# Twelve transformer phases on one core: the output gate turned on TensorE and written to DRAM as rows, late constants and compression weights loaded elsewhere

## Chip, cores, metric

One of the eight cores of a Trainium2 chip. The metric is the device time of one execution in microseconds (us), as the median of several runs. All data is float32.

## The reference

Four blocks of three sublayers each run over 256 tokens of width 1024, twelve sublayers (phases) in all, one after the other. Each adds to the residual x a gated result:

```python
mod = (silu(c) @ ada_w[l] + ada_b[l]).reshape(B, 3, 3, 1, D)     # shift, scale, gate of each sublayer
n = rmsnorm(x, norm_g[l, j]) * (1 + mod[:, j, 1]) + mod[:, j, 0]
x = x + factor * gate(mod[:, j, 2]) * sublayer(n)                # factor 0.5 for j = 0 and 2, else 1
```

gate is 1 + mod in blocks 0 and 1, and mod itself in blocks 2 and 3. Sublayers j = 0 and j = 2 are SwiGLU FFNs, (silu(n @ wi_gate) * (n @ wi_up)) @ wo, with hidden width 2816. Sublayer j = 1 is a mixer: HGRN2 (block 0), differential attention (block 1), and in blocks 2 and 3 native sparse attention beside a spatial-gating MLP. The sparse attention compresses its keys and values with small weights (cmp_w1, cmp_w2). A final rmsnorm ends it. The gate of a sublayer is a vector of 1024 numbers, one for each output channel, the same for all tokens.

## The kernel before

**Phases.** PHASES lists (l, j) for l = 0..3, j = 0..2. (l, 0) and (l, 2) are FFNs, eight in all; (l, 1) are the mixers.

**Weights.** All weights stream from DRAM in pieces of 1 MB (128 x 2048), each as two DMAs of 512 KB, through a ring of three slots, raw. `load` (L354) waits on s_split until the slot's old piece has been cut. For each piece ScalarE copies raw to its high part wH (L504), and VectorE subtracts to get the low part wL (L875), which releases the slot. TensorE then computes each product in three matmuls: high x high (L1530), high x low weights (L1532), low x high (L1534). The last piece of an FFN goes to its own buffers lastH and lastL (L511, L882). All DMAs are issued by the SP queue in program order, so whatever SP waits for holds back everything behind it.

**An FFN.** The hidden width is taken in NF = 11 chunks of 256. A turn takes three pieces: two up pieces (the halves of the contraction over 1024) and one down piece. In turn k TensorE does up(0) for chunk k, then turn_hidden (L1574, four transposes of the hidden chunk k-1 into TM), up(1) for chunk k, and down of chunk k-1. ScalarE copies the turned chunk to hH (L584), and VectorE makes hL (L1010). Chunk 0 and turn 1 are written out, turns 2 to 9 are a hardware loop, turn 10 is written out again, token tile by token tile: turn_hidden, a token tile of up(1), a down tile, turn_tile(0) (L1610), the other token tile, down_last(0), turn_tile(1), a down tile, down_last(1). ScalarE's order there is: cut of up, cut of down chunk 9, cut_last of down chunk 10, hidden_high, cut of the next phase's first piece, then the silu of tile 0 (L592). VectorE's product of tile 0 (L1016) is what turn_tile(0) waits for.

**Modulation.** mod is computed on the side. Matrices of 2 MB a turn (ada, two DMAs of 1 MB) are multiplied with the condition on VectorE (L888), in up to ten turns of an FFN. Each such chunk gives 4 of the 72 columns of a block; a gate takes two chunks.

**The gate.** VectorE computes it as a column tile gcol [128, 8] (gate_column, L932 or L934): element d * 128 + p lies in partition p, column d. The kernel needs it the other way, the same 1024 numbers along the free axis in all partitions (gB [128, 1024]). It goes through DRAM: gate_out (L368) writes gcol to a row of the DRAM tensor gates, and gate_in (L377) waits for that write to land (s_gd), and for the earlier phase's outputs, and reads the row into all 128 partitions:

```python
sp.dma_start(T["gates"][n - 1].rearrange("(d p) -> p d", p=P), gcol[:, :],
             allow_slow_non_contiguous=True).then_inc(s_gd, 16)
```

The order p, d against (d p) makes each of the 1024 elements of four bytes a piece of its own. In an FFN the SP queue has: the loop's loads (the last is the down piece of chunk 9), gate_out, the down piece of chunk 10, gate_in, then the loads of the next phase. In a mixer gate_out stands before the seventh piece and gate_in before the eleventh.

**Late constants** (L416 to L422): a table of 1286 KB, the positions as 256 elements of four bytes, and four vectors read into all partitions. They are issued in (0,0) behind the loop, ahead of gate_out. VectorE waits for them in the first mixer.

**Compression and spatial weights** of blocks 2 and 3 (L476 to L480): cmp_w1 as two DMAs of 1 MB, cmp_w2, gm_ws and two vectors. They are issued ahead of the mixer's first piece.

## Time and profile before

| | |
|---|---|
| median of 3 runs | 2505.46 us (2504.33 to 2522.29) |
| the profiled execution's own time | 2514.27 us |
| its span, first to last instruction | 2512.5 us |
| mean granted TensorE clock | 0.945 of full |
| busy, share of the span: TensorE, VectorE, ScalarE | 91%, 66%, 44% |
| DMA | 537.72 MB, mean 214 GB/s |

An execution's time is its span and 1.8 us around it. PE is the matmuls of TensorE, PEld its weight loads, which overlap them; DVE is VectorE, ACT ScalarE, SPq the queue of SyncE that issues the DMAs. TensorE's matmuls are pipelined, so that a busy PE is not PE at its peak. In a waits row, the engine on the left was idle until the one on the right was done.

### The profile page before, as it was taken

To read this page: it belongs to the slowest core of one execution; us is meant where nothing else is said; L and a number is where in the kernel's file an instruction comes from. 1 tells how busy PE (TensorE), PEld (TensorE's weight loads), DVE (VectorE), ACT (ScalarE), POOL (GpSimd) and SP (SyncE) were. 2 spreads that over 40 slices of the span, in tenths; PEclk is the share of its full clock that TensorE was granted. 3 is DMA by queue.
4 is the path that set the end of the run, shared out by engine and by line. 5 is a ranking of instruction groups with operands and counts; after the bars stand their busy time and mean duration, and the time that the engine had idled before them with its cause. 6 is when DMAs were issued, how large, how long until landed. Compare 5 with 4: busy or idle time off the path is not lost.

```text
span 2512.5 us, 30163 instructions
## 1 busy us (share of the span) xinstructions
PE 2274.6 (91%) x10812; PEld 1888.1 (75%) x10812; DVE 1655.6 (66%) x2305; ACT 1095.3 (44%) x1289; POOL 0.2 (0%) x4
## 2 busy tenths in 40 slices
PE   4997895899899896999899798999989979899998
PEld 3886784688788774788788587778878868777886
DVE  6875667877687686676677554477757756446455
ACT  3443644443444455444433354553444335464433
POOL 0000000000000000000000000000000000000000
PEclk9998997999999996999999897899999989799999
DMA  7987630688698650687698652249768884223554
GB/s 298 332 310 211 165 129 17 227 328 308 198 331 313 200 175 35 217 326 248 189 332 311 209 144 84 101 175 333 284 186 297 308 290 128 101 101 118 184 191 127
DMA packets 140656, 537.72 MB, mean 214 GB/s; under 512 B 27424, under 2 KB 28192, under 8 KB 121504
## 3 DMA queue, kind: packets, MB, share of 16 engines
q1 hardware_dynamic: 140576, 536.64, 62.7%
q8 instruction: 52, 0.85, 0.1%
q14 instruction: 28, 0.23, 0.0%
HBM read 535.49 MB, written 1.10 MB: 214 GB/s over the span
## 4 chain that ended last, share of the span: by engine, by line
PE 73%; DVE 11%; DMA 7%; ACT 6%; issue 2%; SPq 1%; ACTq 0%; DVEq 0%
PE GU L1530 12%; PE GU L1534 11%; PE GU L1532 11%; PE PY L1530 9%; PE PY L1532 9%; PE PY L1534 9%; DVE wL L875 4%; DMA gates<-gcol 3%; ACT wH L504 3%; PE TM L1574 1%; DMA raw<-in_c_w 1%; DMA raw<-in_up_w 1%; PE PY L1777 1%; DVE ada L888 1%; PE PY L1874 1%
## 5 line engine op out<-in xcount | busy, mean ns | idle before, releaser
L875 DVE TENSOR_TENSOR wL<-raw,wH 128x2048 fp32r<-128x2048 f32 x344 | 777.0, 2279 | 284.5 <-ACT wH L504 283.7
L504 ACT ACTIVATE wH<-raw 128x2048 fp32r<-128x2048 f32 x344 | 645.1, 1900 | 237.2 <-PE PY L1534 94.8
L1530 PE MATMUL GU<-wH,xH 128*128 128x512 f32 (+1 forms) x1600 | 640.5, 400 | 40.6 <-DVE xL L997 31.6
L1534 PE MATMUL GU<-wH,xL 128*128 128x512 f32 (+1 forms) x1600 | 627.6, 392 | 0.0
L1532 PE MATMUL GU<-wL,xH 128*128 128x512 f32 (+1 forms) x1600 | 626.9, 392 | 0.0
L1530 PEld LDWEIGHTS GU<-wH,xH 128*128 128x128 f32 x1600 | 304.9, 191 | 109.4 <-issue 29.5
L1534 PEld LDWEIGHTS GU<-wH,xL 128*128 128x128 f32 x1600 | 304.5, 190 | 64.8
L1532 PEld LDWEIGHTS GU<-wL,xH 128*128 128x128 f32 x1600 | 305.3, 191 | 58.8
L888 DVE CUSTOM_DVE_ANT_0 ada<-ada,cond 128x1024 f32<-128x1024 f32 x272 | 316.7, 1221 | 0.0
L584 ACT ACTIVATE hH<-TM 128x512 fp32r<-128x512 f32 x80 | 47.7, 597 | 581.5 <-PE TM L1574 581.5
L1530 PE MATMUL PY<-wH,hH 128*128 128x512 f32 x640 | 203.3, 399 | 39.6 <-DVE hL L1010 38.4
L1010 DVE TENSOR_TENSOR hL<-TM,hH 128x512 fp32r<-128x512 f32 x80 | 55.3, 692 | 239.8 <-ACT hH L584 239.6
L1534 PE MATMUL PY<-wH,hL 128*128 128x512 f32 x640 | 201.3, 396 | 0.0
L1532 PE MATMUL PY<-wL,hH 128*128 128x512 f32 x640 | 200.9, 396 | 0.0
L1530 PE MATMUL PY<-wH,xH 128*128 128x512 f32 x432 | 178.2, 412 | 9.5 <-DVE wL L875 8.1
L1532 PE MATMUL PY<-wL,xH 128*128 128x512 f32 x432 | 173.4, 401 | 0.0
L1534 PE MATMUL PY<-wH,xL 128*128 128x512 f32 x432 | 172.9, 400 | 0.0
L1530 PEld LDWEIGHTS PY<-wH,hH 128*128 128x128 f32 x640 | 120.5, 191 | 69.2 <-issue 41.6
L1534 PEld LDWEIGHTS PY<-wH,hL 128*128 128x128 f32 x640 | 122.6, 192 | 26.2
L1532 PEld LDWEIGHTS PY<-wL,hH 128*128 128x128 f32 x640 | 122.5, 191 | 26.2
L1530 PEld LDWEIGHTS PY<-wH,xH 128*128 128x128 f32 x432 | 85.1, 197 | 29.4 <-issue 5.5
L1534 PEld LDWEIGHTS PY<-wH,xL 128*128 128x128 f32 x432 | 84.2, 195 | 18.6
(293 smaller groups left out, 2079.6 us busy)
## 6 DMA issues: line engine op xcount, KB each, us to landing
raw<-in_up_w SPq DMA_DIRECT2D x352, 512.0 KB, 6.3
ada<-in_ada_t SPq DMA_DIRECT2D x136, 1024.0 KB, 7.9
raw<-in_down_w SPq DMA_DIRECT2D x176, 512.0 KB, 4.7
raw<-in_c_w SPq DMA_DIRECT2D x96, 512.0 KB, 4.5
raw<-in_a_w SPq DMA_DIRECT2D x40, 512.0 KB, 4.5
raw<-in_b_w SPq DMA_DIRECT2D x32, 512.0 KB, 4.8
M<-in_ada_t SPq DMA_DIRECT2D x8, 1024.0 KB, 12.3
gB<-gates SPq DMA_DIRECT2D x12, 512.0 KB, 5.8
```

Source lines behind the costliest of these rows:

```text
L504: act.activation(wH[:, to, 0:words], raw[:, slot, 0:words], ACT.Copy).then_inc(s_high, 1)
L584: act.activation(hH[:, :, :].rearrange("p f s -> p (f s)"), TM[:, 0, :], ACT.Copy).then_inc(s_hh, 1)
L875: dve.tensor_tensor(wL[:, to, 0:words], raw[:, slot, 0:words], wH[:, to, 0:words], ALU.subtract).then_inc(s_split, 1)
L888: ins = dve.tensor_tensor_reduce(w, w, cond[:, :], 1.0, 0.0, ALU.mult, ALU.add, acc[:, 2 * q + b:2 * q + b + 1])
L1010: dve.tensor_tensor(hL[:, :, :].rearrange("p f s -> p (f s)"), TM[:, 0, :], hH[:, :, :].rearrange("p f s -> p (f s)"), ALU.subtract).then_ ...
L1530: pe.matmul(outs[i], aH, wh[i], start=first, stop=False)
L1532: pe.matmul(outs[i], aH, wl[i], start=False, stop=False)
L1534: ins = pe.matmul(outs[i], aL, wh[i], start=False, stop=last)
L1574: ins = pe.transpose(TM[:, 0, f * S + i * P:f * S + (i + 1) * P], sh[:, 1, i, f * P:(f + 1) * P], ident)
L1777: ins = pe.matmul(banks[:, 2 * c + n, 0:P * (tile + 1)], queries[r, h, tile * P:(tile + 1) * P], keys(h)[r, 0:P * (tile + 1)], start=True, ...
L1874: ins = pe.matmul(PY[:, 2, 64 * j:64 * j + 33], w, cT_[:, j, n % 8, n // 8:n // 8 + 33], start=(n == 0), stop=(n == 15))
```

## The change

- gcol has 16 columns. gate_columns takes gate_column's place: in (l, 0) it computes the gates of (l, 0) and (l, 1) at once, in (l, 2) its own. It stands behind the eighth turn of the loop; the mixers compute none.
- In each FFN one more turn is written out of the loops of PE and ACT, turn 9 (the tenth, with chunk 0). After its turn_hidden PE transposes gcol into bank 1 of TM, as 8 or 16 rows of 128; ACT copies that to a new tile gT. DVE's last loop turn becomes a piece of its own as well.
- gate_out writes gT: rows of 128 numbers, 512 bytes, 16 for (l, 0) and 8 for (l, 2). It waits for ACT's copy (s_grow). There are eight such writes; those of the mixers are gone. gate_in reads as before.
- The late constants are issued behind the fifth of (0,0)'s ten ada turns.
- In blocks 2 and 3 the compression weights are issued ahead of the mixer's fifth piece, behind a wait for the outputs of (l, 0), and the spatial weights ahead of the eighth.

```diff
-            def gate_out():
-                n = t.next("gate")
-                sp.wait_ge(s_gcol, n)
-                sp.dma_start(T["gates"][n - 1].rearrange("(d p) -> p d", p=P), gcol[:, :],
-                             allow_slow_non_contiguous=True).then_inc(s_gd, 16)
+            def gate_out(l, j):
+                sp.wait_ge(s_grow, t.next(s_grow))
+                n, rows = 3 * l + j, 2 if j == 0 else 1
+                sp.dma_start(T["gates"][n:n + rows].rearrange("n (d p) -> (n d) p", p=P), gT[0:rows * ND, :]
+                             ).then_inc(s_gd, 16)
...
+            def gate_in(l, j):
+                n = 3 * l + j
+                sp.wait_ge(s_gd, 16 * (2 * l + 1 + j // 2))
+                if n:
+                    sp.wait_ge(s_x, NT * n)
+                sp.dma_start(gB[:, :], T["gates"][n:n + 1].broadcast_to([P, D])).then_inc(s_gb, 16)
+            def load_compression(i):
+                sp.wait_ge(s_x, NT * (3 * i + 7))
+                for k in range(2):
+                    sp.dma_start(w1_[k], T["cmp_w1"][i, k]).then_inc(s_w1, 16)
+                sp.dma_start(w2_[:, :, :], T["cmp_w2_2"][i].rearrange("j f d -> f j d")).then_inc(s_w1, 16)
...
-                    if n == 6:
-                        gate_out()
                     if n == 10:
-                        gate_in()
+                        gate_in(l, 1)
+                    if l > 1 and n == 4:
+                        load_compression(l - 2)
+                    if l > 1 and n == 7:
+                        load_spatial(l - 2)
...
-                if turns:
+                if (l, j) == (0, 0):
+                    loop(1, 5, 1)
+                    late_constants()
+                    loop(6, turns - 5, 1, c0 + 5)
+                elif turns:
                     loop(1, turns, 1)
-                if (l, j) == (0, 0):
-                    late_constants()
...
-                loop(NF - 2)
+                loop(NF - 3)
+                cut()
+                hidden_high()
+                rows = 2 * ND if j == 0 else ND
+                act.wait_ge(s_gt, t.next(s_gt))
+                act.activation(gT[0:rows, :], TM[0:rows, 1, 0:P], ACT.Copy).then_inc(s_grow, 1)
+                cut()
+                cut()
+                silu_gate()
...
+            def gate_columns(l, j):
+                for k in range(2 if j == 0 else 1):
+                    m = (3 * l + j + k) * 3 * ND
+                    factor = 1.0 if k else 0.5
+                    gate, to = mod[:, m + 2 * ND:m + 3 * ND], gcol[:, k * ND:(k + 1) * ND]
...
-                gate_column(l, j)
...
+                loop(NF - 3, turns > 0)
+                gate_columns(l, j)
+                if turns == NF - 1:
+                    c0 = c0 + NF - 3
+                    loop(1, 1)
+                    c0 = c0 + 1
+                else:
+                    loop(1, 0)
...
-                loop(NF - 3)
+                loop(NF - 4)
+                pe.wait_ge(s_h, t.next(s_h))
+                up(0)
+                turn_hidden()
+                rows = 2 * ND if j == 0 else ND
+                pe.wait_ge(s_gcol, t.next(s_gcol))
+                pe.transpose(TM[0:rows, 1, 0:P], gcol[:, 0:rows], ident).then_inc(s_gt, 1)
+                up(1)
+                down(False)
```

The SP queue at the end of (0,0), before; the names are DRAM tensor (in_...) or tile, to<-from, and the semaphores waited for stand in brackets:

```order
L416 DMA cst<-in_table 128x2572
L417 DMA posi<-in_positions 128x2x1
L422 DMA vb<-in_a_onorm 128x128
L422 DMA M<-in_b_qk_g 128x128
L422 DMA M<-in_b_subln 128x128
L422 DMA M<-in_b_lam 128x256
L368 DMA gates<-gcol 128x8x1 [waits s_gcol]
L354 DMA raw<-in_down_w 128x1024 [waits s_split]
L354 DMA raw<-in_down_w 128x1024
L377 DMA gB<-gates 128x1024 [waits s_gd]
L354 DMA raw<-in_a_w 128x1024 [waits s_split]
```

The same place in the changed kernel:

```order
L371 DMA gates<-gT 16x128 [waits s_grow]
L357 DMA raw<-in_down_w 128x1024 [waits s_split]
L357 DMA raw<-in_down_w 128x1024
L380 DMA gB<-gates 128x1024 [waits s_gd]
L357 DMA raw<-in_a_w 128x1024 [waits s_split]
```

The constants have left (they stand between the two loops now), and the gate write takes 16 rows of 128 and waits for s_grow.

ScalarE from the end of its loop to the last cut of (0,0), in the changed kernel (before, the loop is followed at once by the last three of these rows):

```order
L516 ACTIVATE wH<-raw 128x2048 [waits s_eaten,s_raw1]
L596 ACTIVATE hH<-TM 128x512 [waits s_ht]
L637 ACTIVATE gT<-TM 16x128 [waits s_gt]
L516 ACTIVATE wH<-raw 128x2048 [waits s_eaten,s_raw2]
L516 ACTIVATE wH<-raw 128x2048 [waits s_eaten,s_raw0]
L587 ACTIVATE sh<-GU 128x512 [waits s_eaten]
L516 ACTIVATE wH<-raw 128x2048 [waits s_eaten,s_raw1]
L516 ACTIVATE wH<-raw 128x2048 [waits s_eaten,s_raw2]
L523 ACTIVATE lastH<-raw 128x2048 [waits s_raw0]
```

The first six rows are the tenth turn, which was the loop's last; the copy to gT stands between hidden_high and two cuts.

The SP queue at the start of the mixer of block 2, in the changed kernel:

```order
L380 DMA gB<-gates 128x1024 [waits s_x,s_gd]
L357 DMA raw<-in_c_w 128x1024 [waits s_split]
L357 DMA raw<-in_c_w 128x1024
...
L357 DMA raw<-in_c_w 128x1024 [waits s_split]
L357 DMA raw<-in_c_w 128x1024
L386 DMA M<-in_cmp_w 128x2048 [waits s_x]
L386 DMA M<-in_cmp_w 128x2048
L387 DMA w_<-in_cmp_w_2 128x2x64
L357 DMA raw<-in_c_w 128x560 [waits s_split]
```

The first two of the weights M<-in_cmp_w stood directly behind gB<-gates before; now four pieces are ahead of them, and a wait for s_x.

## Rows read from the trace of the kernel before

**Rows 1.** The page: busy time, and the chain by engine.

```profile
PE 2274.6 (91%) x10812; PEld 1888.1 (75%) x10812; DVE 1655.6 (66%) x2305; ACT 1095.3 (44%) x1289; POOL 0.2 (0%) x4
...
PE 73%; DVE 11%; DMA 7%; ACT 6%; issue 2%; SPq 1%; ACTq 0%; DVEq 0%
```

**Rows 2.** Waits: waiting <- waited for: us in total, times, longest us.

```profile
ACT lastH L511 <- DMA raw<-in_down_w: 51.6, 8, 16.2
...
SPq L377 <- DMA gates<-gcol: 82.6, 8, 13.2
```

**Rows 3.** Windows: one loop turn of (0,0); start:end length, then the columns named.

```profile
core 0: us, PE busy (x) PEld busy (x) DVE busy (x) ACT busy (x) POOL busy (x), PEclk, DMA share, GB/s
144.80:161.60 16.80, 16.80 (x78) 13.91 (x77) 12.72 (x15) 6.61 (x5) 0.00 (x0) 1.00 0.86 314
```

**Rows 4.** Windows: ends of the eight FFNs, last turn_hidden to last matmul.

```profile
213.54:249.33 35.79, 20.50 (x83) 15.93 (x82) 12.50 (x18) 10.56 (x15) 0.00 (x0) 0.76 0.63 164
641.72:666.99 25.27, 19.62 (x83) 15.30 (x82) 12.51 (x18) 10.56 (x15) 0.00 (x0) 0.93 0.89 288
841.33:867.36 26.03, 20.90 (x83) 16.12 (x82) 12.48 (x18) 10.56 (x15) 0.00 (x0) 0.87 0.55 191
1200.56:1225.79 25.23, 20.34 (x83) 15.93 (x82) 12.51 (x18) 10.56 (x15) 0.00 (x0) 0.86 0.83 291
1400.38:1437.09 36.71, 22.39 (x83) 17.56 (x82) 13.64 (x18) 12.48 (x16) 0.00 (x0) 0.77 0.63 229
1843.63:1870.56 26.93, 20.84 (x83) 16.38 (x82) 11.35 (x17) 10.56 (x15) 0.00 (x0) 0.87 0.74 268
2044.94:2079.47 34.53, 21.75 (x83) 16.88 (x82) 13.32 (x18) 10.57 (x15) 0.00 (x0) 0.80 0.68 243
2484.94:2505.24 20.30, 17.82 (x81) 14.04 (x79) 10.90 (x16) 6.85 (x13) 0.00 (x0) 1.00 0.29 85
sum 230.79, PE 164.17 PEld 128.14 DVE 99.22 ACT 82.69 POOL 0.00; mean PE 20.52 PEld 16.02 DVE 12.40 ACT 10.34 POOL 0.00
```

**Rows 5.** Timeline, end of (0,2): start, us, engine, line, operation, count, [idle before <- releaser].

```profile
630.45 0.85 SPq L354 DMA_DIRECT2D raw<-in_down_w  x2
...
631.52 0.38 SPq L368 DMA_DIRECT2D gates<-gcol  x1
...
632.51 0.82 SPq L354 DMA_DIRECT2D raw<-in_down_w  x2
...
633.48 2.29 DVE L875 TENSOR_TENSOR wL<-raw,wH 128x2048 fp32r<-128x2048 f32 x1 [0.33 <-ACT wH L504]
...
641.72 0.60 PE L1574 MATMUL TM<-cst,sh 128*128 128x128 f32 x4
...
644.37 0.33 SPq L377 DMA_DIRECT2D gB<-gates  x1
...
646.09 1.91 ACT L511 ACTIVATE lastH<-raw 128x2048 fp32r<-128x2048 f32 x1 [7.64 <-DMA raw<-in_down_w]
...
649.36 0.70 PE L1530 MATMUL PY<-wH,hH 128*128 128x512 f32 x2 [4.28 <-DVE hL L1010]
...
652.61 1.91 ACT L504 ACTIVATE wH<-raw 128x2048 fp32r<-128x2048 f32 x1 [4.12 <-DMA raw<-in_up_w]
...
655.30 0.44 PE L1610 MATMUL TM<-cst,sh 128*128 128x128 f32 x2 [1.36 <-DVE sh L1016]
```

**Rows 6.** Landing of the down pieces issued at 630.45 and at 632.51, us.

```profile
DMA to landing us min/median/max: 4.0/4.4/4.8
...
DMA to landing us min/median/max: 12.3/12.7/13.2
```

**Rows 7.** Chain of waits at the end of (0,2): the next phase's first piece.

```profile
645.22 7.37 DMA raw<-in_up_w
```

**Rows 8.** DMA issues: count, KB each, median us to landing.

```profile
cst<-in_table SPq DMA_DIRECT2D x1, 1286.0 KB, 7.2
...
out<-x SPq DMA_DIRECT2D x2, 512.0 KB, 2.6
```

More of the change, by code:

```diff
@@ L168, in build @@
         scl = sb("scl", [P, ND])
-        gcol = sb("gcol", [P, ND])
+        gcol = sb("gcol", [P, 2 * ND])
+        gT = sb("gT", [2 * ND, P])
         acc = sb("acc", [P, 4])
@@ L273, in build @@
         s_gcol = sem("s_gcol")
+        s_gt = sem("s_gt")
+        s_grow = sem("s_grow")
         s_gd = sem("s_gd")
@@ L362, in load_down, with load_spatial @@
                 load(T["down_w"][l, j // 2][bass.ds(c, 1)].rearrange("c p n -> p (c n)"))
-            def gate_out():
-                n = t.next("gate")
-                sp.wait_ge(s_gcol, n)
-                sp.dma_start(T["gates"][n - 1].rearrange("(d p) -> p d", p=P), gcol[:, :],
-                             allow_slow_non_contiguous=True).then_inc(s_gd, 16)
-            def gate_in():
-                n = t.next("gate", 0)
-                sp.wait_ge(s_gd, 16 * n)
-                if n > 1:
-                    sp.wait_ge(s_x, NT * (n - 1))
-                sp.dma_start(gB[:, :], T["gates"][n - 1:n].broadcast_to([P, D])).then_inc(s_gb, 16)
+            def gate_out(l, j):
[14 more added lines that the diff above has]
+                sp.dma_start(w2_[:, :, :], T["cmp_w2_2"][i].rearrange("j f d -> f j d")).then_inc(s_w1, 16)
+            def load_spatial(i):
+                sp.dma_start(ws_, T["gm_ws"][i].rearrange("t (g s) -> t g s", s=P)).then_inc(s_gm, 16)
+                for k, name in enumerate(("gm_ln_g_2", "gm_ln_b_2")):
+                    sp.dma_start(ln_[:, k, :], T[name][i].unsqueeze(0).broadcast_to([P, 512])).then_inc(s_gm, 16)
             def load_mixer(w, pieces, l):
@@ L432, in ffn, with loop @@
                 c0, turns = ada_turns(l, j)
-                def loop(first, count, with_ada):
+                def loop(first, count, with_ada, c=c0):
                     with sp.Fori(0, count) as i:
@@ L472, in _ @@
                 else:
[L473 to L481 removed]
+                    load_mixer(T["c_w"][l - 2], PIECES_C, l)
             if len(PHASES) == 12:
@@ L618, in loop @@
                     t.leave(count)
-                loop(NF - 2)
+                loop(NF - 3)
[7 more added lines that the diff above has]
+                silu_gate()
+                t.next("done")
                 cut()
@@ L924, in columns @@
                 dve.wait_ge(s_scl, t.next(s_scl))
-            def gate_column(l, j):
-                m = (3 * l + j) * 3 * ND
-                factor = 0.5 if j != 1 else 1.0
-                gate = mod[:, m + 2 * ND:m + 3 * ND]
-                if l < 2:
-                    dve.tensor_scalar(gcol[:, :], gate, 1.0, factor, ALU.add, ALU.mult).then_inc(s_gcol, 1)
-                else:
-                    dve.tensor_scalar(gcol[:, :], gate, factor, None, ALU.mult).then_inc(s_gcol, 1)
+            def gate_columns(l, j):
[3 more added lines that the diff above has]
+                    gate, to = mod[:, m + 2 * ND:m + 3 * ND], gcol[:, k * ND:(k + 1) * ND]
+                    if l < 2:
+                        ins = dve.tensor_scalar(to, gate, 1.0, factor, ALU.add, ALU.mult)
+                    else:
+                        ins = dve.tensor_scalar(to, gate, factor, None, ALU.mult)
+                ins.then_inc(s_gcol, 1)
             def chunk(c):
@@ L1050, in loop @@
                     t.leave(count)
-                done = 0
-                if l == 0:
-                    loop(2, 1)
-                    done, c0 = 2, c0 + 2
-                gate_column(l, j)
-                more = min(turns, NF - 2) - done
-                if more:
-                    loop(more, 1)
-                    done, c0 = done + more, c0 + more
-                if done < NF - 2:
-                    loop(NF - 2 - done, 0)
+                loop(NF - 3, turns > 0)
[4 more added lines that the diff above has]
+                    c0 = c0 + 1
+                else:
+                    loop(1, 0)
                 cut()
@@ L1496, in _ @@
                 boundary(l, j, before, pieces)
-                if j == 1:
-                    gate_column(l, j)
                 if j != 1:
```

17 lines of the change are left out of this document (4 added, 13 removed).

## The prediction

> **What bounds the kernel now.** I read the page's busy line and its chain first, then the waits, then the ends of the eight FFN phases as windows, and last one such end as a timeline.
>
> The page gives TensorE 91% of the span, and the chain is 73% PE [rows 1]. The same line has 7% DMA, and a DMA in the chain of a kernel whose loads are meant to run ahead is something to ask about. The waits answer it [rows 2]: ScalarE waits 51.6 us in 8 cases for the last down piece (lastH), and the SP queue waits 82.6 us in 8 cases for gates<-gcol before it may issue gB<-gates. There are 8 FFN phases, and each has one of either; the other 4 of the 12 gate writes, those in the mixers, are waited for by nobody.
>
> So the loop turns are one thing and the ends of the phases another. In a loop turn PE is busy all 16.80 us at the full clock [rows 3]: nothing gained there on another engine helps. The windows from the last full turn_hidden of a phase to the end of its last matmul [rows 4] have the same work each time, 72 matmuls of 512 columns and 8 transposes (the window counts 83 with neighbours at its edges). They last 20.30 to 36.71 us, 230.79 us together.
>
> What this work takes when nothing holds it: the last window is 20.30 us, at clock 1.00, and PE's busy time in it is 17.82. A loop turn is also 72 matmuls, with 4 transposes; four transposes take 0.60, in the row at 641.72 [rows 5], so 16.80 + 0.60 = 17.4. I take 17.85 as the floor of one end. Eight of them are 142.8, and 230.8 - 142.8 = **88.0 us** are idle time and lowered clock. The other seven windows show PEclk 0.76 to 0.93: of the two levels, 2.4 and 1.2 GHz, the lower one is granted for a part of them, after PE stood idle. That belongs to the 88.0 and goes with the idle time.
>
> **Why these ends are long.** Phase (0,2) is the plain case [rows 5]. SP issues the down piece of chunk 9 at 630.45, the gate write at 631.52 and the down piece of chunk 10 at 632.51. The first lands after 4.4 us, the last after 12.7 [rows 6], with the 1024 four-byte elements of the gate write between them. lastH therefore starts at 646.09, hH and hL behind it, and PE stands 4.28 us before 649.36. Meanwhile SP stands until 644.37, when the gate write has landed (12.85 us after its issue), and only then issues gB and the next phase's first piece. The half issued at 645.22 lands 7.37 later [rows 7], ScalarE's cut of it runs at 652.61, the silu and the product queue behind that, and PE stands again, 1.36 before 655.30.
>
> **The change, part by part.**
>
> *Gate as rows.* Eight writes instead of twelve, of 8 or 16 rows of 512 bytes instead of 1024 or more separate elements. The trace has no such write. Bounds for its landing, G, from its issue: from below, the only other write to DRAM, out<-x with 512 KB, lands in 2.6 us on an empty queue [rows 8], and here 4.2 us are left until the down piece ahead of it is in (630.97 + 4.8 - 631.52); from above, today's 12.85. The write differs from out<-x in being 100 times smaller and from today's in having 64 or 128 times fewer elements, so I stand near the lower end: G about 5.
>
> Then the end of (0,2) goes like this. Down chunk 10 lands near 637.5 (as its neighbour, within 4.8). ScalarE cuts it before 640, ahead of PE's turn_hidden at 641.72, so hH and hL are there when PE asks (it needs hL only after the 12 matmuls of a token tile, 2.7 us later). That wait is gone. What is late next is the next phase's first piece. PE reaches turn_tile at 641.72 + 0.36 + 2.7 + 2.7 = 647.5; from landing to that point today takes 655.30 - 652.59 = 2.7, so the piece must land by 644.8. It lands at 631.52 + G + 0.86 + 7.37 = 639.75 + G, hence in time for G up to 5.1. I take 0.5 us of remaining wait for each of the 7 phases that have a successor: 3.5 us. For G = 12.85 nothing but the queueing of the down piece would be gained.
>
> The Trainium skill bears on G. The page DMA: Bandwidth & Descriptors (Queues, rings and completion order) says that a DMA's semaphore increment is an ordered write, which lands only after every earlier write of that DMA engine. That would be why a 4 KB write holds back whoever waits behind it, and it sets the same 4.2 us under G. The same page (Latency and other measured facts) puts a fixed cost of about 2 us on a DMA because of the round trip of its receipt. Were that to come on top, an estimate from the page is G = 6.2 and 1.1 us of wait in each of 7 phases, and the sum would be some 4 us higher than mine. No run here shows that for such a write yet.
>
> *The hand-over DVE, PE, ACT, SP.* gate_columns stands behind turn 8's product; PE waits for it only after up(0), some 5 us later, so it waits for nothing. On PE 8 transposes are added in a stretch without slack: 0.15 each by the four for 0.60, 1.2 us in all (bounds: 0 and, if each is drained before the next matmul, 0.6 x 8 = 4.8). ACT's copy of 128 columns is under the 0.60 of the 512-column one, and in a loop turn ACT is busy 6.61 of 16.80 [rows 3]. If that cover were gone it would cost 8 x 0.3 = 2.4. Behind it wait two cuts, whose halves DVE takes 1 us later. SP waits for s_grow before the gate write, and behind it stand the last down piece and gB; the copy is done about 5 us before SP arrives there (turn_hidden of that turn is 16.8 before 641.72, SP arrives at 631.4). 0.
>
> *Mixers.* Four gate writes leave the SP queue; nobody waited for them [rows 2], and the pieces behind them were not what PE waited for. 0, at best a few us.
>
> *Late constants* go from the end of (0,0) to behind its fifth turn. The end of (0,0) is 35.79 against 25.27, 26.03 and 25.23 of the three with no such loads [rows 4]: 10.3 us, part of the 88.0 already. What they cost at the new place: the DMA engines are busy 0.86 there [rows 3], so the 1286 KB table (7.2 us to landing [rows 8]) delays the next pieces. Upper bound 10.3 as at the old place; lower 0. What covers it: a piece's low half is ready at 633.48 + 2.29 = 635.8 and PE asks for it after 641.72, 6 us of slack [rows 5]. One table's delay is about that. I take 1.
>
> *Compression weights* go from ahead of the next phase's first piece to behind its fourth. They are in the two windows of 36.71 and 34.53, again within the 88.0. At the new place 2 MB are issued while the DMA queue is nearly empty, well ahead of their first use; 0, at most 3 each.
>
> **Sum.** -88.0 + 3.5 + 1.2 + 1.0 = -82.3 us. The profiled execution took 2514.27 us (span 2512.5 and 1.8 around it), so the changed one would take 2432.0. The median of the runs, 2505.46, lies 8.8 below the profiled execution; carried over, 2423.2. The idle parts may be a little shorter in an unprofiled run, so I say 2425.
>
> **Rivals.**
>
> *A second slow link remains.* The reads right behind gB stay slow, or G is 8.5: the first piece of the next phase is then 3.4 late in 7 phases, 24 instead of 3.5: 2445. For it: gB itself reads one 4 KB row 128 times. Against it: my 7.37 was measured with gB ahead.
>
> *The write is as slow as before*, because what is slow is a write among reads, not the small element. Then only the constants (10.3) and the compression weights (36.71 + 34.53 - 2 x 25.5 = 20.2) give anything: 2505.5 - 30.5 + 2.2 = 2477. For it: every gate write in the trace is of four-byte elements, so the two can't be told apart. Against it: out<-x.
>
> *Slower: PE waits for instructions.* The tenth turn is now written out, some 60 more PE instructions in each of 8 phases, fetched by the DMA engines that the loads keep 0.86 busy. If each needs a fetch that queues like the down piece of [rows 6], 12.7 us, this is 102 us, and 2525. It decides from 88 / 8, about 10 us a phase. Against it: PE already leaves its loop for written-out code 8 times and goes from turn to end without a pause (no idle is shown at 641.72). The Trainium skill, Runtime: NRT & Kernel Launch (Instruction fetch mechanics), says that straight-line code is fetched ahead and that taken branches are what stalls, which would make this rival 0 us; the trace agrees as far as it goes.
>
> **How the numbers follow.** Forecast 0.70, second slow link 0.16, write as slow as before 0.10, slower 0.02, something else of no account 0.02. A measurement of this kernel tells about 1% (25 us) from no change. All but the last two are faster by more: faster 0.96, same 0.02, slower 0.02. The range: below, no wait left and no cost of constants, 2505.5 - 88.0 + 1.2 = 2418.7, and a few us from the mixers, 2411; above, the second slow link with the upper bound of the constants and of the transposes in part, 2451. What it leaves out is the 2477 and the slower case.
>
> **What would show it.** In the changed profile the eight windows should be 17.5 to 19 us at clock 1.00; SP's wait for gates near 5 us or absent; no wait of lastH for a DMA; lastH before turn_hidden. Windows of 21 to 22 with the wait at the next phase's first cut mean the second slow link; a gate write that lands in over 10 us means the second rival; PE idle put down to issue inside the tenth turn means the third. A loop turn of (0,0) longer than 17 us after the fifth would be the late constants. I would be wrong most simply if PE's ends shrank and the norm stretch after them grew by as much.

## The result, and the profile after

| | before | after |
|---|---|---|
| median | 2510.08 us (2504.33 to 2522.29, 4 runs) | 2422.66 us (2420.58 to 2425.39, 4 runs) |
| the profiled execution, its span | 2514.27, 2512.5 | 2420.58, 2418.8 |
| mean granted TensorE clock | 0.945 | 0.959 |

The ratio is 0.9646, with a 95% interval of 0.9605 to 0.9687: 3.5% faster. The forecast was 2425, in a range of 2411 to 2451. The spans of the two profiled executions differ by 93.7 us. Two executions far outside all others, one of the kernel before (9737.65 us) and one of e3 (8289.38 us), are left out of the medians and ratios below.

The page of after, its busy line and its chain, beside [rows 1]:

```profile
PE 2242.5 (93%) x10820; PEld 1868.6 (77%) x10820; DVE 1654.5 (68%) x2305; ACT 1097.5 (45%) x1297; POOL 0.2 (0%) x4
...
PE 80%; DVE 11%; ACT 6%; DMA 2%; issue 1%; SPq 0%; ACTq 0%; DVEq 0%
```

DMA's share of the chain fell from 7% to 2%. PE has eight instructions more (the transposes) and 32 us less busy time: a matmul at the lower clock counts as longer, and there are fewer of those.

The two waits of [rows 2], in after:

```profile
ACT lastH L523 <- DMA raw<-in_down_w: 8.4, 7, 2.4
...
SPq L380 <- DMA gates<-gT: 19.9, 8, 3.5
```

They were 51.6 and 82.6. What is left is no loss in itself: ScalarE stands up to 2.4 us before lastH and still starts it 0.9 us or more ahead of TensorE's turn_hidden.

The eight ends, the same windows as [rows 4], columns as there:

```profile
212.69:230.91 18.22, 17.77 (x83) 14.38 (x82) 12.49 (x18) 8.76 (x14) 0.00 (x0) 1.00 0.56 190
622.97:640.50 17.53, 17.53 (x83) 14.46 (x82) 12.49 (x18) 8.95 (x15) 0.00 (x0) 1.00 0.89 320
814.97:832.50 17.53, 17.53 (x83) 14.46 (x82) 12.49 (x18) 8.78 (x14) 0.00 (x0) 1.00 0.56 196
1163.89:1183.20 19.31, 17.78 (x83) 14.39 (x82) 11.35 (x17) 9.03 (x15) 0.00 (x0) 1.00 0.91 316
1357.67:1375.27 17.60, 17.60 (x83) 14.46 (x82) 12.49 (x18) 8.78 (x14) 0.00 (x0) 1.00 0.56 194
1779.94:1797.50 17.56, 17.56 (x83) 14.46 (x82) 11.34 (x17) 9.69 (x15) 0.00 (x0) 1.00 0.87 325
1971.99:1989.52 17.53, 17.53 (x83) 14.46 (x82) 12.49 (x18) 8.78 (x14) 0.00 (x0) 1.00 0.58 201
2393.95:2411.52 17.57, 17.57 (x81) 14.12 (x79) 10.07 (x15) 5.54 (x13) 0.00 (x0) 1.00 0.05 17
sum 142.85, PE 140.87 PEld 115.18 DVE 95.21 ACT 68.30 POOL 0.00; mean PE 17.61 PEld 14.40 DVE 11.90 ACT 8.54 POOL 0.00
```

Read each row for two things: whether PE's busy time equals the window, and PEclk. Six of the eight are filled by PE, at clock 1.00 in all of them; only (0,0) and (1,2) have idle time, 0.45 and 1.53. The sum went from 230.79 to 142.85, 87.9 less, which is 94% of the 93.7. The rest of the span, 2281.71 before and 2275.9 after (span less the ends), gave 5.8.

The end of (0,2), beside [rows 5]; the gate write stands at 612.82 now:

```profile
611.75 0.85 SPq L357 DMA_DIRECT2D raw<-in_down_w  x2
...
612.82 0.34 SPq L371 DMA_DIRECT2D gates<-gT  x1
...
613.80 0.83 SPq L357 DMA_DIRECT2D raw<-in_down_w  x2
...
616.71 0.33 SPq L380 DMA_DIRECT2D gB<-gates  x1
...
621.23 1.92 ACT L523 ACTIVATE lastH<-raw 128x2048 fp32r<-128x2048 f32 x1 [1.52 <-DMA raw<-in_down_w]
...
622.97 0.60 PE L1592 MATMUL TM<-cst,sh 128*128 128x128 f32 x4
...
625.23 1.92 ACT L516 ACTIVATE wH<-raw 128x2048 fp32r<-128x2048 f32 x1 [1.03 <-DMA raw<-in_up_w]
...
628.88 0.38 PE L1628 MATMUL TM<-cst,sh 128*128 128x128 f32 x2
```

SP issues gB 3.89 us after the gate write (12.85 before), lastH starts 1.7 us ahead of turn_hidden (4.4 behind it before), and no PE row carries an idle time.

### The profile page after: what moved, and what is told of

Read it like the earlier page. It is cut to its first block, busy times and chain, and to the rows that moved or that the text cites. A ratio compares the mean times of both kernels' runs of the same rounds, so it can differ in the third digit from the quotient of the medians.

```text
span 2418.8 us, 30049 instructions
## 1 busy us (share of the span) xinstructions
PE 2242.5 (93%) x10820; PEld 1868.6 (77%) x10820; DVE 1654.5 (68%) x2305; ACT 1097.5 (45%) x1297; POOL 0.2 (0%) x4
## 4 chain that ended last, share of the span: by engine, by line
PE 80%; DVE 11%; ACT 6%; DMA 2%; issue 1%; SPq 0%; ACTq 0%; DVEq 0%
PE GU L1548 13%; PE GU L1552 13%; PE GU L1550 13%; PE PY L1548 10%; PE PY L1550 10%; PE PY L1552 10%; DVE wL L896 4%; ACT wH L516 2%; PE TM L1592 1%; ACT M L568 1%; PE GU L1990 1%; PE PY L1900 1%; ACT xH L563 1%; DMA M<-in_ada_t 1%; DVE x L969 1%
## 5 line engine op out<-in xcount | busy, mean ns | idle before, releaser
L1552 PEld LDWEIGHTS PY<-wH,xL 128*128 128x128 f32 x432 | 83.3, 193 | 18.2
```

The costliest lines, as they stand in the source:

```text
L1552: ins = pe.matmul(outs[i], aL, wh[i], start=False, stop=last)
```

## The experiments

"Ends" are the eight windows in the profiled execution, "between" its span less the ends. Ratios are against the kernel before on the same chip, with 95% intervals.

**Which part of the change gives what.** Three kernels: the rows alone, the moves alone, and the changed kernel with nothing undone but the shape of the write.

e1_rows_only, the changed kernel with the constants and the weights at their old places:

```diff
-                    loop(1, 5, 1)
-                    late_constants()
-                    loop(6, turns - 5, 1, c0 + 5)
+                    loop(1, turns, 1)
+                    late_constants()
...
-                    if l > 1 and n == 4:
-                        load_compression(l - 2)
-                    if l > 1 and n == 7:
-                        load_spatial(l - 2)
```

> The changed kernel with the late constants and the compression weights back at their old places. Theory one (the four-byte elements of the gate write hold the queue): nearly all of the gain stays. The windows of the FFN ends with no such loads are 17.5 as in the changed kernel; only the end of (0,0) and those of (2,0) and (3,0) are longer, by what the loads take ahead of the next piece: at most 10 in (0,0), 3 to 10 each in the other two. Total 2430 to 2445. Theory two (what was slow is a write among reads, and the moves gave the gain): 2470 to 2485.

Measured: 2446.67 us, ratio 0.9737 (0.9696 to 0.9778), ends 168.86. Three of its ends:

```profile
213.77:239.47 25.70, 20.25 (x83) 15.93 (x82) 12.49 (x18) 10.56 (x15) 0.00 (x0) 0.87 0.66 223
...
631.75:649.29 17.54, 17.54 (x83) 14.46 (x82) 12.50 (x18) 8.96 (x15) 0.00 (x0) 1.00 0.88 319
...
1365.12:1393.21 28.09, 20.09 (x83) 16.13 (x82) 12.50 (x18) 8.76 (x14) 0.00 (x0) 0.82 0.62 242
```

Only the ends that have other loads in them are still long: (0,0) 25.70, (2,0) 28.09 and (3,0) 26.81, together 28 us over three ends of 17.54; the other five took 17.54 to 18.05. The time is 1.7 us above the 2430 to 2445 that I expected.

e2_moves_only, the kernel before with those two moves and the old write, in its old places:

```diff
-                if turns:
-                    loop(1, turns, 1)
-                if (l, j) == (0, 0):
-                    late_constants()
+                if (l, j) == (0, 0):
+                    loop(1, 5, 1)
+                    late_constants()
+                    loop(6, turns - 5, 1, c0 + 5)
+                elif turns:
+                    loop(1, turns, 1)
...
+                    if l > 1 and n == 4:
+                        load_compression(l - 2)
+                    if l > 1 and n == 7:
+                        load_spatial(l - 2)
```

> The kernel before with only the late constants and the compression weights moved; twelve gate writes of four-byte elements as before. Theory one: the five ends without such loads stay at 25 to 27 us, the ends of (0,0), (2,0) and (3,0) fall to the same 25 to 27, 28 us less in all: 2475 to 2487. Theory two: 2425 to 2440.

Measured: 2484.57 us, ratio 0.9888 (0.9850 to 0.9927), ends 205.51. Its end of (0,0):

```profile
213.65:240.21 26.56, 21.20 (x83) 16.61 (x82) 12.49 (x18) 10.56 (x15) 0.00 (x0) 0.87 0.56 192
```

Here (0,0) is 26.56, (2,0) 26.33 and (3,0) 24.31, down from 35.79, 36.71 and 34.53 [rows 4]. Four of the other five stay at 25.5 to 27.1, and no end has other loads in it any more. The last end, which the edit does not touch, rose from 20.30 to 23.97; with the same old write it is 20.62 in e3 and 25.27 in e8, so a single end of that kind can differ by 5 us between executions. Within that the parts add up: rows 61.9 off the ends, moves 25.3, together 87.2, and the whole change 87.9.

e3_four_bytes, the changed kernel with everything in it, the written-out turn, the transposes and the copy, but the write made from gcol again:

```diff
-                sp.dma_start(T["gates"][n:n + rows].rearrange("n (d p) -> (n d) p", p=P), gT[0:rows * ND, :]
-                             ).then_inc(s_gd, 16)
+                sp.dma_start(T["gates"][n:n + rows].rearrange("n (d p) -> p (n d)", p=P), gcol[:, 0:rows * ND],
+                             allow_slow_non_contiguous=True).then_inc(s_gd, 16)
```

> The changed kernel, but the gate write takes gcol in elements of four bytes (1024 or 2048) at the very same place, with the same waits; the transpose and the copy to gT are still made. The write's element size alone differs. Theory one: SP waits 10 to 13 us again in each of 8 phases (more in the four with 2048 elements), the FFN ends are 25 us or more, 2480 to 2495. If element size is not it: 2420 to 2426.

Measured: 2484.77 us (three executions), ratio 0.9892 (0.9842 to 0.9941), ends 207.61: the time of e2. Its ends of (0,0), (0,2) and (1,0), and SP's wait:

```profile
213.87:242.57 28.70, 20.55 (x83) 15.94 (x82) 13.10 (x18) 10.56 (x15) 0.00 (x0) 0.82 0.59 200
634.98:660.42 25.44, 19.52 (x83) 15.37 (x82) 12.50 (x18) 10.56 (x15) 0.00 (x0) 0.93 0.84 291
834.91:863.66 28.75, 20.06 (x83) 16.02 (x82) 12.59 (x18) 10.57 (x15) 0.00 (x0) 0.82 0.63 199
```

```profile
SPq L380 <- DMA gates<-gcol: 74.8, 8, 11.9
```

The ends of (l, 0), which write 2048 elements, are 27.4 to 28.7, and those of (l, 2), with 1024, are 20.6 to 25.4. SP's eight waits are 9.4 us each on average and 11.9 at most, a little shorter than the 10 to 13 that I expected. So all of the gain that the moves do not give, 64.7 us of the ends, is in this one statement, and the remodelled turn, which e3 keeps, gives none of it. This is where the rival "the write is as slow as before" falls: it held that a write among reads is slow whatever its shape.

**Must it be rows of 512 bytes?** e4_32_bytes is the kernel before with one statement changed: each partition writes its eight numbers as one piece of 32 bytes, so 128 pieces and no transpose. This leaves out the order of the channels: gB then holds the gates permuted.

```diff
-                sp.dma_start(T["gates"][n - 1].rearrange("(d p) -> p d", p=P), gcol[:, :],
-                             allow_slow_non_contiguous=True).then_inc(s_gd, 16)
+                sp.dma_start(T["gates"][n - 1].rearrange("(p d) -> p d", p=P), gcol[:, :]).then_inc(s_gd, 16)
```

> The kernel before, but the gate write stores each partition's 8 numbers side by side: 128 rows of 32 bytes instead of 1024 of four, at the same twelve places, with no transpose (the channels of the gate then stand in another order). If the number of elements sets the cost, an eighth of today's excess is left: landing 5 to 6.5 us, the plain ends 17.5 to 19, and with the constants and weights at their old places 2435 to 2450. If everything well under 512 bytes is slow in the same way, landing stays over 9 us and the total over 2480.

Measured: 2448.31 us, ratio 0.9744 (0.9728 to 0.9760), ends 169.56, as e1 (0.9737). The ends of (0,2) and (1,0):

```profile
631.75:649.50 17.75, 17.75 (x83) 14.38 (x82) 12.50 (x18) 9.27 (x15) 0.00 (x0) 1.00 0.89 321
823.87:842.38 18.51, 17.79 (x83) 14.39 (x82) 12.51 (x18) 8.89 (x15) 0.00 (x0) 1.00 0.57 195
```

Pieces of 32 bytes give what rows of 512 bytes give. The page counts 129824 packets in the loads' queue (q1) where before has 140576; the 10752 fewer are twelve times 1024 less 128, so the pieces went out as the statement says.

e5_ladder tries four sizes from 32 to 256 bytes. It is the changed kernel, with the copy to SBUF leaving a gap of one element after each k, so that the write falls into pieces of 4k bytes; k is 8 in block 0, 16, 32 and 64 in blocks 1, 2 and 3.

```diff
+        RUN = {(0, 0): 8, (0, 2): 8, (1, 0): 16, (1, 2): 16, (2, 0): 32, (2, 2): 32, (3, 0): 64, (3, 2): 64}
+        def gT_view(l, j, rows):
+            k = RUN[l, j]
+            return gTs[0:rows, 0:P // k * (k + 1)].rearrange("r (a k) -> r a k", k=k + 1)[:, :, 0:k]
...
+                sp.dma_start(T["gates"][n:n + rows].rearrange("n (d a k) -> (n d) a k", a=P // RUN[l, j], k=RUN[l, j]),
+                             gT_view(l, j, rows * ND), allow_slow_non_contiguous=True).then_inc(s_gd, 16)
```

> The changed kernel with the gate write cut into smaller elements, another size in each block: 32 bytes in block 0 (256 and 128 elements), 64 in block 1 (128 and 64), 128 in block 2 (64 and 32), 256 in block 3 (32 and 16). If the number of elements counts, SP's wait for the write is under 4 us everywhere and a little longer only in (0,0), and the total is 2420 to 2428. If there is a step below 512 bytes, all eight waits are longer than the changed kernel's (19.9 us in all).

Measured: 2421.51 us in one execution, ends 141.18, and no size stands out. The page counts 624 packets more than in after, which is 720 pieces in place of 96 rows. (0,0) and (0,2), with 256 and 128 pieces of 32 bytes:

```profile
212.93:231.16 18.23, 17.75 (x83) 14.38 (x82) 12.49 (x18) 8.76 (x14) 0.00 (x0) 1.00 0.56 191
623.59:641.12 17.53, 17.53 (x83) 14.45 (x82) 12.49 (x18) 9.02 (x15) 0.00 (x0) 1.00 0.89 320
```

**Count, size, or neighbourhood?** Before and e4 differ in the size of a piece, in their number and in where they lie. e9_size_and_count puts an extra write, to a DRAM tensor that nobody reads, ahead of the changed kernel's gate write, in another form in each phase. It comes from a tile of constants. The three numbers of EXTRA are the pieces per partition, their width and their pitch in DRAM, both in elements of four bytes.

```diff
+                m, width, pitch = EXTRA[l, j]
+                to = T["spare"][l * 2 + j // 2][0:m * P * pitch].rearrange("(m p w) -> p m w", p=P, w=pitch)
+                src = vec[:, 0:m * (width + 1)].rearrange("p (m w) -> p m w", w=width + 1)
+                sp.dma_start(to[:, :, 0:width], src[:, :, 0:width], allow_slow_non_contiguous=True
+                             ).then_inc(s_spare, 16)
```

> The changed kernel with one more write, to a spare tensor, just ahead of each gate write; nobody reads it. Blocks 0 and 1: 128, 256, 512 and 1024 elements of four bytes. Blocks 2 and 3: 1024 elements of 8, 16, 32 and 64 bytes. The changed kernel's ends are 17.5 us, so each window shows what its write costs. If the cost goes by the number of elements: it grows over the first four (from 0 to about 8 us) and stays at about 8 in the last four. If it goes by the four bytes: it grows over the first four and falls to 0 over the last four, at the latest at 32 bytes.

Measured: 2453.21 us in one execution.

| phase | pieces, side by side | landing of the extra write, us | the end, us |
|---|---|---|---|
| (0,0) | 128 of 4 bytes | 8.6 | 23.19 |
| (0,2) | 256 of 4 | 9.2 | 23.25 |
| (1,0) | 512 of 4 | 11.7 | 24.48 |
| (1,2) | 1024 of 4 | 11.4 | 24.64 |
| (2,0) | 1024 of 8 | 7.5 | 21.74 |
| (2,2) | 1024 of 16 | 6.8 | 18.39 |
| (3,0) | 1024 of 32 | 5.3 | 17.59 |
| (3,2) | 1024 of 64 | 5.0 | 17.56 |

The window rows of 1024 pieces of four bytes and of 1024 pieces of 32:

```profile
1183.31:1207.95 24.64, 20.08 (x83) 16.06 (x82) 11.44 (x17) 10.56 (x15) 0.00 (x0) 0.86 0.84 295
...
2001.76:2019.35 17.59, 17.59 (x83) 14.40 (x82) 12.49 (x18) 8.76 (x14) 0.00 (x0) 1.00 0.62 214
```

At 1024 pieces the size decides: 32 bytes are free, 4 bytes cost 7 us of the end. And the count alone does not: 1024 pieces of 32 bytes cost nothing while 128 of four cost 5.6. Neither branch of my expectation fits the first four rows: from 128 to 1024 pieces of four bytes the cost grows only from 5.6 to 7.1, not from 0 to 8. But the sizes also differ in how many pieces share 32 bytes of DRAM, eight, four, two or one. e10_pitch keeps 1024 pieces of 4 bytes throughout and changes only the pitch, in two phases each:

```diff
-        EXTRA = {(0, 0): (1, 1, 1), (0, 2): (2, 1, 1), (1, 0): (4, 1, 1), (1, 2): (8, 1, 1),
-                 (2, 0): (8, 2, 2), (2, 2): (8, 4, 4), (3, 0): (8, 8, 8), (3, 2): (8, 16, 16)}
+        EXTRA = {(0, 0): (8, 1, 1), (0, 2): (8, 1, 8), (1, 0): (8, 1, 16), (1, 2): (8, 1, 128),
+                 (2, 0): (8, 1, 1), (2, 2): (8, 1, 16), (3, 0): (8, 1, 128), (3, 2): (8, 1, 8)}
```

> As the run before, but always 1024 elements of four bytes, and another distance between them in DRAM: side by side, 32, 64 and 512 bytes apart in the phases (0,0), (0,2), (1,0) and (1,2), and side by side, 64, 512 and 32 apart in (2,0), (2,2), (3,0) and (3,2). If what is slow is that neighbours in one stretch of DRAM are each read, changed and written back, one behind the other, the write is slow only side by side (and perhaps at 32) and the windows with 64 and 512 bytes stay at 17.5 to 19. If each small element is slow for itself, all eight windows are 22 to 29 us.

Measured: 2437.49 us in one execution.

| pitch of the 1024 elements | landing, us | the two ends, us |
|---|---|---|
| side by side | 11.6, 11.9 | 24.43, 24.81 |
| 32 bytes | 5.8, 5.5 | 17.53, 17.56 |
| 64 bytes | 5.8, 5.6 | 19.40, 17.57 |
| 512 bytes | 5.6, 5.4 | 18.16, 18.49 |

Side by side and 32 bytes apart, the windows and, below, the landing rows of the two extra writes:

```profile
212.51:236.94 24.43, 20.54 (x83) 15.98 (x82) 12.50 (x18) 10.55 (x15) 0.00 (x0) 0.86 0.62 208
629.35:646.88 17.53, 17.53 (x83) 14.46 (x82) 12.49 (x18) 8.77 (x14) 0.00 (x0) 1.00 0.95 329
```

```profile
DMA to landing us min/median/max: 11.6/11.6/11.6
...
DMA to landing us min/median/max: 5.8/5.8/5.8
```

The same 1024 elements of four bytes, 32 bytes apart, cost nothing. So neither the size of a piece nor the number of pieces makes the old write slow, but that its pieces lie closer together than that: side by side, eight of them share 32 bytes of DRAM. That the stretch in which they hurt one another is just 32 bytes is a reading of both tables and not shown by itself. Pieces of 8 and 16 bytes side by side land after 7.5 and 6.8 us and those of 32 after 5.3, but no pitch between 4 and 32 was tried for the four-byte elements. The ends of 18.2 to 19.4 in the lower half of the table are 0.6 to 1.9 us over 17.54, where side by side costs 7. They are of the kind that (1,2) shows in after (below): in (1,0), with 19.40, PE stands 1.64 us for the next phase's first piece.

The Trainium skill, DMA: Bandwidth & Descriptors (Specifications), wants transfers of at least 512 bytes for the full rate, because a smaller one is done as a read and a write back. Were that a step at 512 bytes which shows here, e4 and e5 would have been slow in every end. They were not: 17.5 to 18.5, but for the three ends of e4 with the other loads in them. The four-byte elements 32 bytes apart would have been slow too, and they landed in 5.5 to 5.8. Collectives: The Full Stack (Rules for kernel authors) names 32 bytes as the alignment that avoids such a read and write back, for the buffers of a collective; e9 and e10 fit that size, in another setting. Why neighbours hurt one another stays open: in all the slow forms they come from different partitions, and small pieces side by side from one partition were not tried.

**Do the next loads lose by SP's standing, or by the write itself?** In the kernel before SP stands 82.6 us for the gate write, with the next phase's first piece behind it. e8_before_read_later lets that piece go first, in the kernel before, and e7_gate_read_later does the same in the changed one. The lines are e7's:

```diff
-                gate_in(l, j)
+                if (l, j) == PHASES[-1]:
+                    gate_in(l, j)
...
             def ffn(l, j):
                 load_up(l, j, 0, 0)
+                if j == 0 and l:
+                    gate_in(l - 1, 2)
```

(and in a mixer behind its first piece).

> The kernel before, but with gate_in (SP's wait for the write and the read into gB) behind the next phase's first piece. This takes away only that SP stands ahead of that piece; the four-byte write stays in the queue. If SP's standing were the whole cost, the second wait of each end (28 us in all with its clock) and most of the excess go: under 2460. By theory one the down piece of chunk 10 and the next piece still land late, behind the write: the plain ends fall from 25 to 22 or 23, 10 to 25 us in all: 2480 to 2495.

Measured: 2504.65 us, ratio 0.9967 (0.9955 to 0.9978), ends 225.52. I expected 2480 to 2495; this was a clear miss. Its end of (0,2), and ScalarE's rows there, show why:

```profile
639.46:666.29 26.83, 20.33 (x83) 16.21 (x82) 12.50 (x18) 10.56 (x15) 0.00 (x0) 0.87 0.85 275
```

```profile
646.05 1.91 ACT L516 ACTIVATE lastH<-raw 128x2048 fp32r<-128x2048 f32 x1 [9.85 <-DMA raw<-in_down_w]
...
648.55 1.91 ACT L509 ACTIVATE wH<-raw 128x2048 fp32r<-128x2048 f32 x1
```

The cut of the next piece at 648.55 waits for nothing any more, where it waited 4.12 us at 652.61 [rows 5]. But lastH starts only at 646.05, 6.6 us behind the turn_hidden of this end (639.46), where it was 4.4 behind. Its piece was issued at 630.25, directly behind the gate write as before, and lands after 14.2 to 15.4 us, where it was 12.3 to 13.2 [rows 6]. The piece that was let go ahead is under way at the same time, 13.4 to 14.6 us. Whether it delays the down piece is not shown: lastH starts 0.4 to 2.2 us later against turn_hidden than before in all eight ends, but also by 2.2 in the last, where the order is as it was. PE stands 6.50 us for hL instead of 4.28, and the end took 26.83 us instead of 25.27. So the write holds back the loads issued behind it, and SP's standing is the small part. The ends fell by 5.3 us (230.8 to 225.5); in the seven in which the order was changed it is 10.2 us, since the last end, left as it was, rose from 20.30 to 25.27. The median fell by 7.8.

> The changed kernel, but the read of the gate into gB (and SP's wait for the write) stands behind the next phase's first piece instead of ahead of it. If the wait left in the ends of (0,0) and (1,2), 0.45 and 1.53 us, is that piece behind the slow read of gB, both windows become 17.5 and the time falls by 2.4 us, to about 2420; gB is needed only some 10 us later and is no new wait. If it is the write's landing that is left, nothing changes.

Measured: 2425.71 us, ratio 0.9648 (0.9609 to 0.9687), ends 140.39, all eight between 17.54 and 17.57. The two ends that I expected to shorten did, but the time was to be about 2420. e12_read_later_again is the same kernel once more, beside the changed kernel on the same chip, e11_changed_again, in five rounds.

> The changed kernel unaltered, beside the next run on the same chip: 2420 to 2426. Its mixer stretches, in the runs so far 401.7 to 409.4 us for the one of block 2 with the same idle time, go by the time at the lower clock, about 1.6 us for each step of 3.4 us, so they tell nothing of an edit.

> The kernel of e7 again: the gate read behind the next phase's first piece, all eight FFN ends at 17.5. If the 2.5 us that this gave in the ends reach the time, it is 2418 to 2424 and below e11; if the mixers' clock gives them back each time, as in e7, it is 2423 to 2427.

Measured: e11 2424.96 us (2420.22 to 2426.81), ratio 0.9665 (0.9641 to 0.9689), ends 142.35; e12 2421.62 us (2420.67 to 2424.01), ratio 0.9656 (0.9632 to 0.9679), ends 140.30. The profiles show the remaining wait gone from the ends in both pairs, 2.5 us from after to e7 and 2.1 from e11 to e12, and every end of e12 at 17.53 or 17.54, such as (1,2), where after has 19.31:

```profile
1165.59:1183.13 17.54, 17.54 (x83) 14.46 (x82) 11.29 (x17) 9.61 (x15) 0.00 (x0) 1.00 0.87 316
```

In time the two can't be told apart (0.9656 against 0.9665, with intervals of 0.0024 either way). In the ends of e12 PE has no idle time left.

**Is the 5.8 us outside the ends due to the four writes that left the mixers?** e6_mixer_writes puts four writes of 1024 elements side by side back into the mixers' queue, to a tensor that nobody reads, in the changed kernel.

```diff
                     if n == 10:
                         gate_in(l, 1)
...
+                    if n == 6:
+                        sp.dma_start(T["spare"][l].rearrange("(d p) -> p d", p=P), gcol[:, 0:ND],
+                                     allow_slow_non_contiguous=True).then_inc(s_spare, 16)
```

> The changed kernel with four extra writes of 1024 four-byte elements to a spare tensor, where the mixers' gate writes used to stand; nobody reads them. The stretches of the four mixers lost 5.1 us against the kernel before, which I had put at 0. If that came from the write's traffic slowing the loads behind it, the stretches grow back by 4 to 6 us. If it came from something else (a different order of instructions, chance), they stay.

Measured: 2425.13 us, ratio 0.9648 (0.9632 to 0.9664), ends 143.94, between 2282.28. Taken alone, 2282.28 against the 2275.90 of after looks like the answer. It is not: e7, without any such write, has 2283.54. Beside them stand e11 with 2280.19, e5 with 2278.51 and e3, with its old write but none in the mixers, 2275.39. And e2 and e8, which keep all four mixer writes of the kernel before, have 2276.69 and 2277.36. The stretch from the end of (2,0) to that of (2,2) shows what differs. Before, after, e6, e7 and e3, one row each:

```profile
1437.09:1843.63 406.54, 387.07 (x1904) 324.05 (x1903) 253.48 (x408) 188.69 (x240) 0.00 (x0) 0.93 0.54 182
```

```profile
1375.27:1779.94 404.67, 385.41 (x1905) 322.69 (x1904) 253.24 (x407) 189.74 (x242) 0.00 (x0) 0.94 0.55 194
```

```profile
1379.54:1787.23 407.69, 388.39 (x1905) 325.13 (x1904) 253.32 (x407) 189.32 (x242) 0.00 (x0) 0.93 0.57 193
```

```profile
1375.67:1785.04 409.37, 390.06 (x1904) 326.70 (x1903) 253.25 (x407) 189.64 (x242) 0.00 (x0) 0.92 0.54 192
```

```profile
1424.33:1826.43 402.10, 383.63 (x1903) 321.09 (x1903) 253.19 (x407) 188.87 (x241) 0.00 (x0) 0.94 0.55 191
```

The idle time of PE is the same in all, length less busy, 18.5 to 19.5. The busy time goes with the clock: by the trace's record of the clock 44.4 us of that stretch are at the lower level, 1.2 GHz, in e3, 51.2 in after, 54.6 in before, 58.0 in e6 and 61.4 in e7. The same holds for all fourteen traces: their lengths of this stretch, 402.1 to 409.4, stand in the order of their time at the lower level, 44.4 to 61.4. The same kernel differs too: 404.67 in after, 406.35 in e11. So this stretch follows the granted clock from execution to execution and no edit tried here. That the four writes cost nothing is consistent with it, but a cost of 1 or 2 us would not be seen.

## Why the prediction was right

**What bounds.** The ends of the FFNs were the place: 87.9 of 93.7 us came from them, against 88.0 of idle time and lowered clock counted ahead. With the floor as measured (below) there were 90.5 to gain, and 2.5 are left.

**The floor of an end** was put at 17.85 and is 17.54: 17.53 to 17.60 in the six ends of after that PE fills, and 17.53 or 17.54 in all eight of e12. The 17.4 of the other way of working it out was the nearer. 8 x 0.31 = 2.5 us more than forecast.

**The gate as rows.** G was put near 5. The chain of after shows it for (1,2), with what hangs on it:

```profile
1153.75 5.41 DMA gates<-gT
...
1160.03 8.75 DMA raw<-in_up_w
1168.80 1.92 ACT wH L516
```

In (0,2) gB is issued 3.89 us after the write, and so G is no more there. The fixed cost of about 2 us, which the Trainium skill gives in DMA: Bandwidth & Descriptors (Latency and other measured facts) and which would have made G an estimated 6.2 on top of the 4.2, does not show as an addition: the trace has 3.9 to 5.4. The deadline of 5.1 was about right too: the only end with more than 0.7 us of wait is the one with 5.41. But there the larger part is the piece's own landing, 8.75 where I carried over the 7.37 of [rows 7]. That is what the rival "a second slow link" was about, in one end of seven and with 1.8 us. Which end it is changes: in e11, the same kernel, (1,2) takes 17.57 and (0,2) 19.07, and there G is 5.15 and the piece lands after 8.80. The remaining waits are 0.7 in (0,0) and 1.8 in (1,2) over the floor, 2.5 against the 3.5 of the sum. One sign named ahead did not come: lastH still waits for its DMA, 8.4 us in seven ends, because the last down piece of (0,2) lands after 5.6 to 7.0 us and not within 4.8. It cost nothing, since lastH still starts ahead of turn_hidden.

**The hand-over.** The turn with the transpose: from turn_hidden of turn 9 at 606.06 to that of turn 10 at 622.97 are 16.91 us, against 16.81 in before (624.91 to 641.72). So a transpose costs 0.10 and not 0.15, 0.8 us in all instead of 1.2. No wait for the copy shows on SP.

**Late constants.** The table is issued at 118.36 and lands after 7.3 us. The window of (0,0) with both in it, and the next two:

```profile
112.00:128.80 16.80, 16.80 (x79) 13.91 (x78) 12.72 (x14) 6.61 (x5) 0.00 (x0) 1.00 0.80 296
128.80:145.60 16.80, 16.80 (x79) 13.89 (x77) 10.73 (x11) 6.72 (x5) 0.00 (x0) 1.00 0.92 376
145.60:162.40 16.80, 16.80 (x79) 13.91 (x78) 14.68 (x18) 6.72 (x5) 0.00 (x0) 1.00 0.86 324
```

PE is busy throughout, 16.80 as in [rows 3], while the DMA rate rises to 376 GB/s behind the table. The two pieces issued behind it land after 8.4 to 10.4 and 10.6 to 11.6 us, where a piece of such a turn in the kernel before took 6.1 to 6.8, and the slack of 6 us that the prediction counted takes it. The cost is 0, not 1.

**Compression weights.** The prediction put 10.3 and 20.2 us, 30.5 together, on what these loads cost at their old places: e1 has 28 left in the same three ends, and e2 takes 29.8 off them. e2 gains only 25.3 over all eight, mostly because its last end is 23.97 and not 20.30.

**Mixers**, 0 in the sum: the profiled difference outside the ends is 5.8. The runs above spread over 8 us there with and without the mixers' writes, and the one stretch followed through goes with the clock; that the whole 5.8 is the clock's is likely and not shown.

**The sum** by steps, forecast and found: ends -88.0 + 3.5 + 1.2 = -83.3, found -87.9; constants 1.0, found 0; outside 0, found -5.8. The profiled execution was to take 2432.0 and took 2420.58, 11.4 less. The median was to be 2425 and is 2422.66. Part of the nearness is luck: the 8.8 us between the old profiled execution and its median became 4.2 as a fourth run came in (2514.27 against 2510.08), and with those the forecast would have been 2427.8. The other part is that two errors cancel: the sum was 11.4 too small between the profiled executions, and the 8.8 carried over to the median was too much, since the median of after lies 2.1 above its profiled execution.

**The rival that TensorE waits for instructions** (2525): six of the eight ends are filled by PE, the other two wait for a piece of weights, the written-out turn takes 16.91, and the instruction queue moved five packets more. The queue's rows of the page, before and then after:

```profile
q8 instruction: 52, 0.85, 0.1%
```

```profile
q8 instruction: 57, 0.93, 0.2%
```

That agrees with what the Trainium skill, Runtime: NRT & Kernel Launch (Instruction fetch mechanics), says of straight-line code.

**One expectation failed outright**, that of e8. It named the landing of the two pieces behind the write as the cost, which held. But it still gave SP's standing 10 to 25 us, with plain ends of 22 or 23, and they were 23.5 to 26.8: the down piece [rows 6] landed no earlier, and it alone keeps PE waiting. SP's 82.6 us are a large number beside the cost and not the cost.

## What to carry to other kernels

Before turning a layout on an engine to get long rows for a small write to DRAM, see how far apart its pieces start in DRAM: here pieces of 32 bytes, or even four bytes at a pitch of 32, cost as little as rows of 512, while four bytes side by side cost 7 us an end. A small write in a queue of large loads is paid for by the loads behind it, so look at their landing and not at who waits for the write. And hold the parts of the span that the change does not touch, with their time at either clock, beside those of other runs of the same kernel before giving it their difference.

## What was not expected of the hardware

- 4 KB written side by side in four-byte pieces, behind a load of 1 MB, take 11.4 to 11.9 us to land in e9 and e10 (12.8 in the end of (0,2) before), and 5.4 to 5.8 at a pitch of 32, 64 or 512 bytes.
- While such a write is under way, the DMA engines are busy and move little. A window of the kernel before, in the end of (0,2), and then one of e10 with the elements 32 bytes apart:

```profile
636.00:644.00 8.00, 8.00 (x38) 6.60 (x38) 6.81 (x10) 1.92 (x1) 0.00 (x0) 1.00 1.13 77
```

```profile
621.00:627.00 6.00, 6.00 (x28) 4.99 (x27) 5.90 (x8) 1.99 (x2) 0.00 (x0) 1.00 1.02 310
```

  The share adds up the time that packets took, and so can pass 1. Near 1 with 77 GB/s beside it, it is a blockage, and with 310 GB/s it is work. The share alone would have told nothing.
- The same stretch of the same work took 402.1 to 409.4 us with the same idle time of TensorE, by how long the lower clock was granted in it.
